# Second mixer: low-rank unit fifth and values last in the stream, preparation of the pairs between the units, shift in one VectorE operation, key root per head

## The reference

```python
p = h @ w_in                                   # 512 x 2816
ps, pc = p[..., :D_SHIFT], p[..., D_SHIFT:]
ps = ps + (token_shift(ps) - ps) * shift_mu    # r, k, v, xw, xa, xg
d = w0 + tanh(xw) @ w_up;  decay = exp(-exp(-0.5) * sigmoid(d))
a = sigmoid(a0 + xa @ a_up);  g = sigmoid(xg) @ g_up
kk = heads(k * k_k)
kk = kk * rsqrt(maximum(sum(kk * kk, axis=-1, keepdims=True), 1e-12))
k = k * (1.0 + (a - 1.0) * k_a)
y = rwkv7_recurrence(r, decay, k, v, -kk, kk * a)   # per head, frame by frame
y = group_norm(y) + sum(r * k * r_k, axis=-1, keepdims=True) * v
out_a = y * g
glu = pc[..., :512] * sigmoid(pc[..., 512:])
out_b = silu(layernorm(causal_conv_31_taps(glu) + conv_b))
return concatenate([out_a, out_b], axis=-1) @ w_out
```

## Time and profile before

| | us |
|---|---|
| runs | 3702.51, 3702.67, 3705.03 |
| median | 3702.67 |
| profiled execution | 3696.74 |
| its span | 3695.1 |
| busy: TensorE matmul / VectorE / ScalarE | 3479.5 / 2001.3 / 1122.0 |
| mean granted TensorE clock | 0.976 |
| second mixer: units projected | 1480.2 to 1600.1 |
| preparation of the pairs | 1600.1 to 1668.7 |
| pairs | 1668.7 to 1796.4 |
| to the output projection's first product | 1843.6 |

### The profile page before, as it was taken

One profiled execution on the slowest core, in us unless ns is written; L12 is line 12 of the kernel. 1 busy time (PEld: TensorE's weight loads), 2 busy tenths in 40 slices (PEclk: granted clock), 3 DMA queues, 4 the chain that ended last, 5 costly groups with the idle time before them and its releaser, 6 DMA issues. The chain is left out here.

```text
span 3695.1 us, 45654 instructions
## 1 busy us (share of the span) xinstructions
PE 3479.5 (94%) x18472; PEld 2718.8 (74%) x18478; DVE 2001.3 (54%) x2662; ACT 1122.0 (30%) x1465; POOL 154.0 (4%) x128
## 2 busy tenths in 40 slices
PE   7999999999999999957799999999999989999998
PEld 6887776688878886837578886765788866568886
DVE  5667545522354334897753335696434348953334
ACT  2222335322232223232332223325322233452222
POOL 0000000000000000000000000330000012300000
PEclk8999999999999999979899999999999999999999
DMA  6554221122222222210012222210222221102221
GB/s 225 190 183 171 80 105 46 57 91 102 91 80 93 101 92 87 92 46 4 2 69 91 102 91 80 80 69 24 82 100 93 100 80 69 58 35 103 91 103 68
DMA packets 47213, 325.64 MB, mean 88 GB/s; under 512 B 5232, under 2 KB 5488, under 8 KB 8672
## 3 DMA queue, kind: packets, MB, share of 16 engines
q1 hardware_dynamic: 41792, 290.10, 22.0%
q0 software_dynamic: 5280, 33.52, 2.5%
HBM read 321.51 MB, written 2.10 MB: 88 GB/s over the span
## 5 line engine op out<-in xcount | busy, mean ns | idle before, releaser
L1991 PE MATMUL PS<-HH,WH 128*128 128x512 f32 x2264 | 895.2, 395 | 25.5 <-DVE HL L2392 18.9
L2374 DVE TENSOR_TENSOR WL<-RAW,WH 128x2048 fp32r<-128x2048 f32 x264 | 613.7, 2325 | 503.8 <-ACT WH L2227 498.2
L1992 PE MATMUL PS<-HL,WH 128*128 128x512 f32 x2264 | 884.8, 391 | 0.0
L1993 PE MATMUL PS<-HH,WL 128*128 128x512 f32 x2264 | 884.6, 391 | 0.0
L2227 ACT ACTIVATE WH<-RAW 128x2048 fp32r<-128x2048 f32 x264 | 503.1, 1906 | 330.2 <-PE PS L1993 322.1
L1991 PEld LDWEIGHTS PS<-HH,WH 128*128 128x128 f32 x2264 | 427.2, 189 | 140.6 <-issue 33.1
L1993 PEld LDWEIGHTS PS<-HH,WL 128*128 128x128 f32 x2264 | 427.0, 189 | 90.8
L1992 PEld LDWEIGHTS PS<-HL,WH 128*128 128x128 f32 x2264 | 427.3, 189 | 87.5 <-issue 1.2
L1991 PE MATMUL PS<-AH,WH 128*128 128x512 f32 x1056 | 412.3, 390 | 3.3 <-DVE A L2440 3.0
L1992 PE MATMUL PS<-AL,WH 128*128 128x512 f32 x1056 | 411.4, 390 | 0.0
L1993 PE MATMUL PS<-AH,WL 128*128 128x512 f32 x1056 | 411.3, 390 | 0.0
(11 more groups left out here) (395 smaller groups left out, 3668.2 us busy)
## 6 DMA issues: line engine op xcount, KB each, us to landing
RAW<-in_w SPq DMA_DIRECT2D x264, 1024.0 KB, 4.8
E<-in_ada POOLq DMA_DIRECT2D x28, 1024.0 KB, 5.0
E<-in_ada SPq DMA_DIRECT2D x4, 1024.0 KB, 11.8
G<-in_ada SPq DMA_DIRECT2D x4, 1024.0 KB, 19.3
X<-in_x SPq DMA_DIRECT2D x1, 2048.0 KB, 13.7
out_x<-A SPq DMA_DIRECT2D x8, 256.0 KB, 2.1
G<-in_cos POOLq DMA_DIRECT2D x4, 256.0 KB, 3.2
G<-in_sin POOLq DMA_DIRECT2D x4, 256.0 KB, 3.4
```

Source lines behind the costliest of these rows:

```text
L1991: nc.tensor.matmul(out, wh, xh, start=start, stop=False)
L1992: nc.tensor.matmul(out, wh, xl, start=False, stop=False)
L1993: return nc.tensor.matmul(out, wl, xh, start=False, stop=stop)
L2374: nc.vector.tensor_tensor(WL[:, w % 2, :], RAW[:, w % 2, :], WH[:, w % 2, :].bitcast(F32), ALU.subtract).then_inc(w_lo, 1)
```

## The change

- The unit order becomes: 4 convolution units, low rank, k, k, r, r, v, v. The column index of mu follows by `mu_of`, the target tile by `chunk_of`.
- Chunks use banks 0 to 3 in turn (the last unit 6 and 7); banks 4 to 7 take the preparation's products. A unit waits for the gate product or the shift of the unit two before it.
- ScalarE evacuates a chunk times (1 - mu) to its target; VectorE adds mu times the chunk of the frame before, read from PSUM: one operation, without a wait for its own landing.
- The preparation's steps are placed after units 4 to 9 on each engine. TensorE: decay after unit 5, rate after 6, key sums after 7, spread after 8, bonus after 9. The key's squares are summed per head into 32 rows (`SEL2`), floor and root are 128 x 512 once, and a second product spreads the (negated) root over the head's channels (`SPREAD2`).
- Work that goes from VectorE to ScalarE: k times k_k, the factor of k (`t2`), r_k (put into `RKB2`), the copy of the bonus. The decay before a frame is read as the shifted `DEC2`, so one subtraction and one exponential go.
- `scaled` is 4 operations for each pair. `pe_pairs` waits for scaled of its pair alone.
- The last unit's shift, its weight split for unit 12 and bonus times values move into pair 0.
- Taps alternate between channel groups, each waiting for the landing of its own group's last tap. 89 stand in the stream (`TAPS_IN`), 35 in the pairs (`TAPS_LEVEL`).

The diff, cut to its core. Lines of before that are removed are shown only where they are short; the others are in the functions printed above.

```diff
@@ -92,7 +92,7 @@
         "mix1": [("f1", 1), ("u1", 2), ("v1", 2), ("q1", 2), ("k1", 2), ("va1", 2)],
-        "mix2": [("pc2", 4), ("r2", 2), ("k2", 2), ("v2", 2), ("lora2", 1)],
+        "mix2": [("pc2", 4), ("lora2", 1), ("k2", 2), ("r2", 2), ("v2", 2)],
         "mix3": [(f"ik3_{layer}", 1), (f"iq3_{layer}", 1), (f"qa3_{layer}", 2), (f"ka3_{layer}", 2), (f"va3_{layer}", 2),
...
@@ -1189,14 +1189,18 @@
-        RP2 = G[:, 16:21, :].rearrange("p a s -> p (a s)")[:, 0:4 * (S + 1)].rearrange("p (m s) -> p m s", m=4)
-        B2, LW2, KK2, CC2, BV2 = G[:, 0:4, :], G[:, 4:8, :], G[:, 8:12, :], G[:, 12:16, :], G[:, 16:20, :]
-        T2, V2W, R0W, RW = A[:, 0:4, :], A[:, 4:8, :], A[:, 8:12, :], A[:, 12:16, :]
+        B2, KK2 = A[:, 0:4, :], A[:, 4:8, :]
+        INV2, DEC2 = G[:, 16:20, :], A[:, 12:16, :]
+        TMP2 = [E[:, 15, :], E[:, 14, :], G[:, 20, :], G[:, 21, :]]
+        BV2 = [SG[:, 0, :], SG[:, 1, :], V[:], R0[:]]
+        RKB2 = A[:, 20, :]
+        BONUS_BANK, LAST_BANKS = (0, 1, 4, 5), (6, 7)
...
+        SEL2, SPREAD2, OM2 = LEVELS[:, 448:480], LEVELS[:, 480:608], LEVELS[:, 608:626]
...
@@ -1213,14 +1217,17 @@
+        TAPS_IN = [9, 11, 11, 11, 9, 9, 14, 6, 2, 3, 4]
+        TAPS_LEVEL = [(2, 1, 2, 1, 1), (3, 2, 2, 1, 1), (3, 2, 2, 1, 1), (3, 2, 2, 1, 2)]
...
@@ -1295,6 +1302,18 @@
+        def chunk_of(q):
+            return (LO2, XG2)[q] if q < 2 else (K2, R2, V2)[(q - 2) // 4][:, (q - 2) % 4, :]
+        def mu_of(q):
+            return 12 + q if q < 2 else (4, 0, 8)[(q - 2) // 4] + (q - 2) % 4
+        def unit_banks(u):
+            return LAST_BANKS if u == U2 - 1 else (2 * (u % 2), 2 * (u % 2) + 1)
...
@@ -1308,10 +1327,9 @@
-            pool.dma_start(LEVELS[:, 0:7 * CH], T["levels"]).then_inc(m2_loads, 16)
+            pool.dma_start(LEVELS[:, 0:7 * CH + 160], T["levels"]).then_inc(m2_loads, 16)
...
-            pool.memset(RP2[:, :, 0:1], 0.0)
...
@@ -1323,27 +1341,38 @@
+                if 2 <= u < 6:
+                    pe.wait_ge(glu_done, u - 1)
+                elif u >= 6:
+                    pe.wait_ge(shifted, 2 * (u - 6) + 2)
+                h["project"](w + u, unit_banks(u), first=u == 0)
+                if u == 5:
+                    pe.wait_ge(m2_loads, 48)
+                    after("act", "low rank")
+                    for m in range(4):
+                        raise_(mm(PS[4 + m][:], LU2[0:64, m * P:(m + 1) * P], LO2[0:64, :], start=True, stop=True), "decay", m)
+                elif u == 6:
+                    for m in range(4):
+                        after("act", "sig d", m)
+                        raise_(mm(PS[4 + m][:], LU2[64:P, m * P:(m + 1) * P], LO2[64:P, :], start=True, stop=True), "rate", m)
+                elif u == 7:
+                    after("act", "kk sq")
+                    for m in range(4):
+                        last = mm(PS[4][32 * m:32 * m + 32, :], SEL2, TMP2[m], start=True, stop=True)
+                    raise_(last, "kk")
+                elif u == 8:
+                    after("dve", "kk root")
+                    for m in range(4):
+                        rows = slice(32 * m, 32 * m + 32)
+                        raise_(mm(PS[4 + m][:], SPREAD2[rows, :], R[rows, :], start=True, stop=True), "spread", m)
+                elif u == 9:
+                    after("act", "rkb")
+                    after("dve", "rk")
+                    after("dve", "kk")
+                    for m in range(4):
+                        raise_(mm(PS[BONUS_BANK[m]][:], RKB2[:, m * P:(m + 1) * P], TMP2[m], start=True, stop=True), "bonus", m)
...
@@ -1382,6 +1411,10 @@
+                if not a:
+                    after("dve", "scaled", m)
+                if m == 0:
+                    after("act", "bonus", 3)
...
@@ -1471,6 +1504,7 @@
                 after("dve", "hat", m)
+                pe.wait_ge(shifted, CHUNKS2)
                 for x in (3, 2, 0, 1):
...
@@ -1593,41 +1627,62 @@
             act.wait_ge(m2_zero, 1)
+            def evacuate(u):
+                for c in range(2):
+                    q = 2 * (u - 4) + c
+                    ac(chunk_of(q), PS[unit_banks(u)[c]][:], ACT.Copy, scale=OM2[:, mu_of(q):mu_of(q) + 1]).then_inc(proj_evac, 1)
             for u in range(U2):
                 act.wait_ge(w_used, w + u + 1)
...
+                if u < U2 - 1:
+                    split(w + u + 2)
                 if u < 4:
...
                         act.wait_ge(glu_done, u - 1)
...
+                    ac(SG[:, u % 2, :], PS[unit_banks(u)[1]][:], ACT.Sigmoid).then_inc(gate_done, 1)
+                    continue
+                if u == 4:
+                    after("dve", "cols")
+                evacuate(u)
+                if u == 4:
+                    act.wait_ge(shifted, 2)
+                    ac(LO2[0:64, :], LO2[0:64, :], ACT.Tanh)
+                    raise_(ac(XG2, XG2, ACT.Sigmoid), "low rank")
+                elif u == 5:
+                    for m in range(4):
+                        after("pe", "decay", m)
+                        raise_(ac(INV2[:, m, :], PS[4 + m][:], ACT.Sigmoid, bias=col("w0", m)), "sig d", m, landed=False)
+                elif u == 6:
+                    for m in range(4):
+                        after("pe", "rate", m)
+                        raise_(ac(B2[:, m, :], PS[4 + m][:], ACT.Sigmoid, bias=col("a0", m)), "sig a", m, landed=False)
+                    for m in range(4):
+                        act.wait_ge(shifted, 3 + m)
+                        last = ac(KK2[:, m, :], K2[:, m, :], ACT.Copy, scale=col("k_k", m))
+                    raise_(last, "kk raw")
+                    after("dve", "sums", 3)
+                    for m in range(4):
+                        last = ac(TMP2[m], KK2[:, m, :], ACT.Square)
+                    raise_(last, "kk sq")
+                elif u == 7:
+                    after("pe", "kk")
+                    for m in range(4):
+                        last = ac(TMP2[m], B2[:, m, :], ACT.Identity, scale=col("k_a", m), bias=OM2[:, 14 + m:15 + m])
+                    raise_(last, "t2", landed=False)
+                    after("dve", "kk v")
+                    h["chain"](ac(R0[:], R[:], ACT.Ln))
+                    raise_(ac(R0[:], R0[:], ACT.Exp, scale=-0.5), "kk r0", landed=False)
+                    for m in range(4):
+                        last = ac(RKB2[:, m * P:(m + 1) * P], const("blocks"), ACT.Copy, scale=col("r_k", m))
+                    raise_(last, "rkb", landed=False)
+                    raise_(ac(INV2, DEC2, ACT.Exp, scale=DECAY), "inverse")
+                    raise_(ac(DEC2, DEC2, ACT.Exp, scale=-DECAY), "decays", landed=False)
+                elif u == 9:
+                    for m in range(4):
+                        after("pe", "bonus", m)
+                        raise_(ac(BV2[m], PS[BONUS_BANK[m]][:], ACT.Copy), "bonus", m, landed=False)
+            split(w + U2 + 1)
             t.add("w", U2)
...
             def take(to, src, *key):
...
@@ -1699,78 +1754,106 @@
+            raise_(v.tensor_scalar(OM2[:, 0:14], col("mu", 0, 14), -1.0, 1.0, ALU.mult, ALU.add), "cols")
+            chain(v.tensor_scalar(OM2[:, 14:18], col("k_a", 0, 4), -1.0, 1.0, ALU.mult, ALU.add))
+            done, marked, latest = [0, 0, 0, 0], [None] * 4, [3]
+            def convolve(count, ready=4):
...
+                    open_ = [m for m in range(min(ready, 3)) if done[m] < TAPS] or [m for m in (3,) if m < ready and done[m] < TAPS]
+                    open_ = [m for m in open_ if m != latest[0]] or open_
+                    if not open_:
+                        return
+                    m = min(open_, key=lambda x: done[x])
+                    if marked[m] is not None:
+                        chain.until(marked[m])
+                    marked[m] = chain.mark(tap(v, m, done[m]))
+                    done[m] += 1
+                    latest[0] = m
+            def shift(u):
+                for c in range(2):
+                    q = 2 * (u - 4) + c
+                    dest = chunk_of(q)
+                    dve.wait_ge(proj_evac, t("proj") + q + 1)
+                    v.scalar_tensor_tensor(dest[:, 1:], PS[unit_banks(u)[c]][:, 0:S - 1], col("mu", mu_of(q)), dest[:, 1:],
+                                           ALU.mult, ALU.add).then_inc(shifted, 1)
+            def sums():
+                for m in range(4):
+                    after("act", "sig d", m)
+                    raise_(v.tensor_tensor_scan(DEC2[:, m, :], SEG2, INV2[:, m, :], 0.0, ALU.mult, ALU.add), "sums", m, landed=False)
+            def key_root():
+                after("act", "kk r0")
+                chain(v.scalar_tensor_tensor(R[:], R[:], -0.5, R0[:], ALU.mult, ALU.mult))
+                chain(v.tensor_tensor(R[:], R[:], R0[:], ALU.mult))
+                raise_(v.scalar_tensor_tensor(R[:], R[:], 1.5, R0[:], ALU.add, ALU.mult), "kk root", landed=False)
+            def by_frame(x):
+                return x.rearrange("p (c s) -> p c s", s=CH)
+            def scaled(m):
```

(64 more changed lines are left out.)

130 lines of the change are left out of this document (14 added, 116 removed).

## The result

| | before | after |
|---|---|---|
| median of 4 runs, us | 3703.29 (3702.51 to 3705.03) | 3664.91 (3663.82 to 3666.90) |
| ratio | | 0.9900 (95% interval 0.9887 to 0.9912) |
| profiled execution, us | 3696.74 | 3665.18 |
| its span | 3695.1 | 3663.5 |

The change saves 38.4 us in the medians, where 41.1 were forecast. The two profiled executions lie only 31.6 apart, because that of before reached the second mixer early: its first product there starts at 1480.2, that of after at 1485.2, and every other profiled execution of this study, of before's code with an addition too, at 1484.7 to 1487.4. So stages are compared from the mixer's own first product.

The account below looks back on a forecast made before the run. VectorE was taken to bound the 70.7 us preparation behind the projected units. Stream -48.1 plus pairs +7.0 gave -41.1, so 3702.7 - 41.1 = 3661.6 us; forecast 3657 to 3667 (chance 0.62), wide range 3653 to 3673.

Parts of the forecast that it names:

- The bound: Preparation between last unit and first masked read: VectorE is its bound, 70.7 us, the span the change attacks.
- Decay, rate, bonus: Stream: three groups of four full-shape f32 products added to TensorE between units, 3 x 3.55 = 10.65 us.
- Narrow groups: Stream: key sums and spread, 1.0 us each if four products overlap, 3.55 if not; 2.0 together, range 2.0 to 7.1.
- Units behind a group: Stream: a switch of tiling mode drains the engine, but no term stands for it in the sum.
- Wait for the key root: Stream, after unit 8: TensorE waits 3.3 us for VectorE's key root before the spread, range 0.6 to 6.
- Stream and gap together: Up to the first masked read, 6.6 us after the last unit: -70.7 + 10.65 + 2.0 + 3.3 + 6.6 = -48.1 us.
- Pairs: +7.0: Pairs: VectorE work moved in (shift +1.4, split +1.0, bonus times values +1.3, taps +3.3), range 3.5 to 12.
- Taps: 3.3 forecast for seven: Pairs: 35 taps in place of 28, partly hidden in update waits, +3.3 us, range 1.5 to 5.5.
- the clock in the pairs: Start of the pairs after some 7 us idle: no loss, as they began at 0.66 for 11 us before.
- slower rival: Granted clock stays low from the root to the pairs' end: 3743 us, chance 0.02.
- The banks: Stream: VectorE over 5 us behind after unit 6, so four later units wait 4 to 5 us: 3680, chance 0.03.
- second rival: Pairs absorb their extra work, growing only +2.5 us: 3655, chance 0.15.

Follow-up runs that it names:

- e1: Changed kernel with the preparation put back behind the last unit, last shift and split for unit 12 back in the stream: 3685.71 us, ratio 0.9962.
- e8: e5 with three idle products, four taps moved from unit 7 to 8, ScalarE's two wide exponentials behind its split for unit 10: 3655.40 us, ratio 0.9870.
- e6: Changed kernel with seven taps left out of pairs 1 to 3, 28 in the pairs instead of 35: 3663.24 us.
- e5: e4 plus two idle f32 products, results unread, behind the first products of the pairs: 3653.95 us, ratio 0.9868.
- e3: Changed kernel with six idle f32 products, results unread, filling TensorE's gap before the first masked read: 3659.92 us.
- e2: Changed kernel with four taps moved from unit 7, before the key root, to unit 8: 3662.09 us.
- e4: Changed kernel with nine taps (seven behind units 9 and 10, two of pair 0) moved into VectorE's idle times of units 1 to 8: 3658.34 us.
- e9: Kernel before with seventeen idle f32 products while TensorE waits for the preparation's last scaling: 3703.47 us, ratio 1.0006.
- e10: e5 with six taps of pairs 1 to 3 left out: 3654.22 us.

## Why the prediction was nearly right, step by step

**The bound, and what the placement buys.** Right. Of the 70.7 us behind the stream, in which VectorE was the bound, 65 are gone. e1 adds what the prediction didn't split: 21.6 us are the placement of the preparation, 15.6 the changed work and the moved taps together.

**Decay, rate, bonus: 10.65.** Measured 3.63 + 3.63 + 3.03 = 10.3. Right.

**Narrow groups: 1.0 each, if four products run side by side.** Shown. Key sums 1.00; spread 1.07 in e8. In after it was 1.92, because TensorE came out of the 2.78 us wait at the lower level (granted clock 0.53 from 1595.2 to 1597.1, 0.50 up to 1598.5, 1.00 before the wait). So the spread cost 0.9 more than forecast, and the unit behind it began with distances of 0.59 and 0.43 between products instead of 0.23 and took 11.76.

**Units behind a group: 0 in the sum, 2.1 measured.** This is a term that the prediction set at nothing. The first product of a unit behind decay is followed by the next after 0.34 us (1554.29 to 1554.63), normally 0.23, and some tenths follow; 0.3 a unit, and 0.9 for the one after the wait. The Trainium skill, page TensorEngine Tiling (Array Packing), section Key Properties, says that a switch of tiling mode drains the engine; the trace is in accord with 0.1 to 0.3 us at such places, but bonus, which has the units' own full shape, is followed by 0.4 more as well, so the runs don't show the switch to be the cause.

**Wait for the key root: 3.3.** Measured 2.78. The working held in its parts: root finished 14.9 after the key sums' start (1580.21 to 1595.11; forecast 15.1), TensorE there after 12.2 (forecast 11.9). No wait before bonus: VectorE's last key product ends at 1605.45 and TensorE comes at 1608.85, 3.4 of margin instead of 1.3, as spread and unit 9 were slower. VectorE's timeline, from the root to the split for unit 10, and the first masked read:

```profile
1594.42 0.69 DVE L1794 SCALAR_TENSOR_TENSOR R<-R 128x512 f32<-128x512 f32 x1
1596.92 2.29 DVE L2467 TENSOR_TENSOR WL<-RAW,WH 128x2048 fp32r<-128x2048 f32 x1 [1.81 <-ACT WH L2320]
...
1629.19 1.28 DVE L1868 TENSOR_TENSOR G<-PS,CN 128x512 f32<-128x512 f32 x2
```

1.81 for a forecast 1.9, and the first masked read 5.95 after the last unit's end (1623.24 by the cut used here), forecast 6.6. Stream and gap together: forecast -48.1, measured 18.24 - 64.86 = **-46.6**.

**Pairs: +7.0, measured +9.3.** The mechanism was mis-sized in one place and missing in another. Taps: 3.3 forecast for seven; pairs 1 to 3, which hold all seven added ones, give nothing to 2.5 at even clock (e6 against e5, e3 and e2). Pair 0 with shift, split and bonus products: forecast 3.7; VectorE's timeline has the rows foreseen, shift, split and updates:

```profile
1631.85 1.40 DVE L1780 SCALAR_TENSOR_TENSOR E<-PS,PV,E 128x511 f32<-128x511 f32 x2
...
1637.55 2.28 DVE L2467 TENSOR_TENSOR WL<-RAW,WH 128x2048 fp32r<-128x2048 f32 x1
...
1640.42 1.08 DVE L1883 TENSOR_TENSOR G<-G,PS 128x256 f32<-128x256 f32 x3 [0.26 <-PE PS L1458]
```

The wait of 0.60 before the three updates is 0.26 here. Pair 0 took 33.5 us against 29.2, +4.3, but at a clock of 0.82 against 0.94. In e5, at 1.00 and with two taps fewer, it took 30.3.

**The step that failed** is the clock in the pairs, which the prediction put at nothing: "the pairs began at 0.66 for 11 us before as well, so the second is no loss". From the first masked read on, before's pairs ran at 0.74 for 10 us and at 1.00 from there to the end; the change's ran at 0.51 for 10 us, at 0.84 for the next 10, and dipped again in pairs 1 and 2. By pair, from VectorE's first operation on a pair's inverse to the next pair's (2.05 us lie ahead of pair 0 everywhere):

| us (granted clock) | pair 0 | pair 1 | pair 2 | pair 3 |
|---|---|---|---|---|
| before | 29.2 (0.94) | 32.5 (1.00) | 32.7 (1.00) | 29.1 (1.00) |
| after | 33.5 (0.82) | 35.9 (0.96) | 33.2 (0.94) | 30.3 (1.00) |
| e2, gap of 10.0 | 31.6 (0.88) | 34.3 (1.00) | 32.9 (1.00) | 30.8 (1.00) |
| e3, gap filled | 33.4 (0.90) | 33.6 (1.00) | 33.3 (1.00) | 29.5 (1.00) |
| e4, gap of 1.3 | 31.7 (0.89) | 35.8 (0.95) | 33.2 (1.00) | 30.7 (1.00) |
| e5, that filled | 30.3 (1.00) | 32.4 (1.00) | 32.5 (1.00) | 30.5 (1.00) |
| e6, gap of 5.9 | 33.5 (0.83) | 33.6 (1.00) | 32.4 (1.00) | 29.6 (1.00) |

What the runs show in place of that nothing is a cost of single microseconds: 5.7 between e4 and e5. At full clock e5's pairs are 2.1 us over before's, with two taps fewer than the change's, or some 4 with 0.785 for each of the two. So about half of the change's +9.3 or more goes with its clock and not with the work that was moved in. What the runs don't show is that the gap before the pairs is the whole cause. Filling it (e3) gave 5.3 us in the medians and 3.1 to 3.4 in the profile's pairs, but hardly any of it in pair 0; e2, with the longest gap and a start at 0.53, has pairs as short as e3's; e6, with the change's gap and the change's pair 0, has no dip in pair 1. So the +7.0 came nearer than its working, which is luck in part: for the moved work it has more than the 2 to 4 us that this cost at full clock, and the clock is missing from it. The prediction had the mechanism only as its slower rival, all or nothing; it acts in part. That rival itself, a clock low from the root to the pairs' end, didn't come about: units 9 and 10 ran at full pace after the first products, as its own argument said.

**The other rivals.** The banks never held a unit up: no wait before a unit in the list of waits. The pairs absorbed their extra work less than the second rival wanted (+2.5), at the clock they had; at full clock (e5: +2.1, with 33 taps in the pairs) that rival comes close.

**The sum.** Mixer -37.2 for -41.1: stream 2.3 too small, gap 0.7 too large, pairs 2.3 too small; 3.9 in all. Of the stream's 2.3, the restart at the lower clock after the wait makes 1.8 (spread 0.9, the unit behind it 0.9).

**Open.** How much of before's pairs was low clock (e9), what a tap in the pairs costs (e6, e10), and what brings the later dips of after: from pair 1 on, the change, e2, e3, e4 and e5 have the same work, yet pair 1 ran at 0.96, 1.00, 1.00, 0.95 and 1.00.
